# Attention value products: one group per query tile, or one group per branch over up to 512 queries

## The reference, cut to what matters

```python
ss = jnp.einsum('bgrqd,bgqnkd->bgrqnk', qb, k_sel) - slopes[..., None] * d_s
ss = jnp.where(d_s >= 0, ss, NEG)
p_s = jax.nn.softmax(...)
o_s = jnp.einsum('bgrqnk,bgqnkd->bgrqd', p_s, v_sel)
...
return gb[0] * o_c + gb[1] * o_s + gb[2] * o_w
```

## Time and profile before

| | us |
|---|---|
| median of 3 runs (1801.71 to 1802.36) | 1801.89 |
| the profiled execution's own time | 1800.54 |
| its span in the profile | 1798.7 |
| PE busy, share | 1764.1, 98% |
| DVE busy, share | 1222.4, 68% |
| ACT busy, share | 711.9, 40% |
| PE busy in 1290 to 1384 | 83.96 of 94.00 |
| DVE busy there | 79.05 |
| ACT busy there | 74.66 |

### The profile page before, as it was taken

The page is one execution under the profiler, slowest core; times in us unless marked ns, Lnnn a source line. Parts: engine busy times, 40 slices in busy tenths (PEclk is TensorE's granted clock), DMA queues, the critical chain, the costliest instruction groups (busy, mean ns, idle before and its releaser), DMA issues.

```text
span 1798.7 us, 23469 instructions
## 1 busy us (share of the span) xinstructions
PE 1764.1 (98%) x8780; PEld 1426.4 (79%) x8780; DVE 1222.4 (68%) x1784; ACT 711.9 (40%) x964; POOL 164.9 (9%) x40
## 2 busy tenths in 40 slices
PE   7999999999999999999999999999999999999998
PEld 7896888888887988688888888787756878888886
DVE  5367786877877555868886877863787545555556
ACT  5323442332433513353332332646786532222222
POOL 0000000000000000000000000000101344444442
PEclk9999999999999999999999999999999999999999
DMA  6330334333332243123334333253400222222221
GB/s 270 118 114 27 138 110 148 120 117 140 117 121 91 92 131 104 61 105 134 125 122 144 117 117 140 72 173 111 110 13 1 94 71 95 97 101 101 96 94 70
DMA packets 30991, 194.23 MB, mean 108 GB/s; under 512 B 5456, under 2 KB 5840, under 8 KB 8656
## 3 DMA queue, kind: packets, MB, share of 16 engines
q1 hardware_dynamic: 22752, 156.77, 24.9%
q10 hardware_dynamic: 8176, 36.58, 6.1%
HBM read 187.04 MB, written 2.11 MB: 105 GB/s over the span
## 4 chain that ended last, share of the span: by engine, by line
PE 91%; DVE 4%; issue 2%; ACT 2%; DMA 1%; POOL 0%; DVEq 0%; ACTq 0%; SPq 0%; PEldq 0%
PE ps L486 28%; PE ps L488 28%; PE ps L487 28%; PE ps L630 1%; PE ps L644 1%; DMA raw<-in_weights 1%; DVE pb L2218 1%; PE ps L652 0%; PE ps L614 0%; PE ps L899 0%; PE ps L809 0%; DVE wl L1709 0%; DMA x<-in_xin 0%; ACT pt L1480 0%; DVE nt L1677 0%
## 5 line engine op out<-in xcount | busy, mean ns | idle before, releaser
L486 PE MATMUL ps<-xh,wh 128*128 128x512 f32 x1440 | 567.4, 394 | 13.6 <-DVE xl L1662 9.5
L488 PE MATMUL ps<-xh,wl 128*128 128x512 f32 x1440 | 561.4, 390 | 0.0
L487 PE MATMUL ps<-xl,wh 128*128 128x512 f32 x1440 | 561.0, 390 | 0.0
L1057 ACT ACTIVATE wh<-raw 128x2048 fp32r<-128x2048 f32 x143 | 273.6, 1915 | 451.3 <-DMA raw<-in_weights 446.7
L486 PEld LDWEIGHTS ps<-xh,wh 128*128 128x128 f32 x1440 | 270.7, 188 | 73.2 <-issue 14.6
L487 PEld LDWEIGHTS ps<-xl,wh 128*128 128x128 f32 x1440 | 270.9, 188 | 56.8 <-issue 1.7
L488 PEld LDWEIGHTS ps<-xh,wl 128*128 128x128 f32 x1440 | 270.6, 188 | 56.7
L1709 DVE TENSOR_TENSOR wl<-raw,wh 128x2048 fp32r<-128x2048 f32 x109 | 249.0, 2285 | 93.0 <-ACT wh L1057 93.0
L459 POOL TENSOR_TENSOR wl<-raw,wh 128x2048 fp32r<-128x2048 f32 x35 | 161.2, 4608 | 1605.8 <-ACT wh L1057 1507.8
L2307 DVE TENSOR_TENSOR ymix<-ymix,ps 128x512 f32<-128x512 f32 x112 | 74.3, 682 | 149.5 <-PE ps L488 144.8
L486 PE MATMUL ps<-wh,ah 128*128 128x512 f32 x432 | 170.8, 395 | 1.6 <-DVE al L1935 1.2
(11 more groups left out here) (292 smaller groups left out, 2189.4 us busy)
## 6 DMA issues: line engine op xcount, KB each, us to landing
raw<-in_weights SPq DMA_DIRECT2D x144, 1024.0 KB, 4.8
adab<-in_ada ACTq DMA_DIRECT2D x22, 1024.0 KB, 4.8
t<-in_cst ACTq DMA_DIRECT2D x1, 3200.0 KB, 10.3
turned<-q ACTq DMA_DIRECT2D x8, 256.0 KB, 4.0
turned<-k ACTq DMA_DIRECT2D x8, 256.0 KB, 4.1
adab_tail<-in_ada ACTq DMA_DIRECT2D x2, 1024.0 KB, 9.3
out_y<-x SPq DMA_DIRECT2D x8, 256.0 KB, 2.0
raw<-in_weights SPq DMA_DIRECT2D x2, 512.0 KB, 6.6
```

The costliest lines, as they stand in the source:

```text
L486: pe.matmul(out, w_hi, m_hi, start=start, stop=False)
L487: pe.matmul(out, w_hi, m_lo, start=False, stop=False)
L488: return pe.matmul(out, w_lo, m_hi, start=False, stop=stop)
L1057: act.activation(wh[:, s, :], raw[:, s, :], ACT.Copy).then_inc(hi_made, 1)
```

## The change

The transposed weights of one whole branch are kept: `pt` grows from two slots of one unit to one area of four key tiles by 512 queries for each g. It lies over the parts of `xh` and `xl` that hold channels 512 to 1023, whose last readers are the projections ahead of attention. K(U) writes the columns of its query tile. The value products of v = 0 to 3 run as one group behind T of v = 4, those of v = 4 to 7 as one group behind T of v = 8, and the compressed ones, now `compressed_values`, behind T of v = 0 of the next round, where they were. In a group, key tile j takes the queries from j * 128 to 511 in one matmul for each g, so a branch has 8 matmuls (16 records). `pt` may be overwritten only when the group before has read it: K of v = 0 and 4 waits for key tile 0 of that group, K of v = 1 and 5 for all of it (`values_before`).

```diff
+        xh_at = top[0]
         xh = keep("xh", [P, KT, S], F32R)
+        assert top[0] == xh_at + size([P, KT, S])
         xl = keep("xl", [P, KT, S], F32R)
...
-        pt = at("pt", [P, 2, 2, NT, P], F32, big + 28672)
+        pt = at("pt", [P, 2, KT, S], F32, xh_at + size([P, 4, S]))
...
+        def values_before(U):
+
+            r, v = divmod(U, 9)
+            if v == 8:
+                return 5 * r
+            return 5 * r + (0 if v >= 4 else -3) + (1 if v % 4 == 0 else 2)
...
-            def values(U):
-
-                r, v = divmod(U, 9)
-                pe.wait_ge(pt_evac, U + 1)
-                if v == 0 and r >= 2:
+            def values(r, b):
+
+                pe.wait_ge(pt_evac, 9 * r + 4 * b + 4)
+                if b == 0 and r >= 2:
                     pe.wait_ge(att_evac, r - 1)
-                i, b = v % 4, v // 4
-                for j in range(i + 1) if v < 8 else (0,):
+                for j in range(NT):
                     for g, h in enumerate(halves):
-                        if v < 8:
-                            last = pe.matmul(ps[h, 6 + r % 2, i * P:(i + 1) * P], vv[:, j, b * P + HD * g:b * P + HD * g + HD],
-                                             pt[:, U % 2, g, j, :], start=(v == 0), stop=False)
-                        else:
-                            last = pe.matmul(ps[h, 6 + r % 2, :], vcs[0:N_CMP, HD * g:HD * g + HD], ptc[0:N_CMP, g, :],
-                                             start=False, stop=True)
+                        last = pe.matmul(ps[h, 6 + r % 2, j * P:S], vv[:, j, b * P + HD * g:b * P + HD * g + HD], pt[:, g, j, j * P:S],
+                                         start=(b == 0 and j == 0), stop=False)
+                    if j in (0, NT - 1):
+                        last.then_inc(values_used, 1)
+
+            def compressed_values(r):
+
+                pe.wait_ge(pt_evac, 9 * r + 9)
+                for g, h in enumerate(halves):
+                    last = pe.matmul(ps[h, 6 + r % 2, :], vcs[0:N_CMP, HD * g:HD * g + HD], ptc[0:N_CMP, g, :], start=False, stop=True)
                 last.then_inc(values_used, 1)
...
                 turn(U)
-                if U:
-                    values(U - 1)
-            values(UNITS - 1)
+                r, v = divmod(U, 9)
+                if v in (4, 8):
+                    values(r, v // 4 - 1)
+                if U and v == 0:
+                    compressed_values(r - 1)
+            compressed_values(3)
...
                 act.wait_ge(t_done, U + 1)
-                if U >= 2:
-                    act.wait_ge(values_used, U - 1)
+                if v in (0, 1, 4, 5, 8) and values_before(U) > 0:
+                    act.wait_ge(values_used, values_before(U))
                 if v < 8:
-                    w = (v % 4 + 1) * P
-                    act.activation(pt[:, U % 2, :, 0:v % 4 + 1, :], ps[:, 4:6, 0:w].rearrange("p g (j t) -> p g j t", t=P), ACT.Copy)                       .then_inc(pt_evac, 1)
+                    i = v % 4
+                    act.activation(pt[:, :, 0:i + 1, tokens(i)], ps[:, 4:6, 0:(i + 1) * P].rearrange("p g (j t) -> p g j t", t=P), ACT.Copy)\
+                       .then_inc(pt_evac, 1)
...
-                act.wait_ge(values_used, 9 * r + 9)
+                act.wait_ge(values_used, 5 * r + 5)
```

## The result

| us | before | after |
|---|---|---|
| median, 5 runs of each | 1801.89 | 1815.44 |
| lowest to highest | 1801.08 to 1802.57 | 1809.95 to 1815.97 |
| profiled execution's own time | 1800.54 | 1815.97 |

The ratio is 1.0071, with a 95% interval of 1.0059 to 1.0082: **slower by 13.5 us**, where 6.4 were forecast. The sign was right; the forecast size was about half of what was measured, and the median lies outside the stated range of 1803 to 1811. The runs of the changed kernel also scatter: four lie at 1814.6 to 1816.0 with a mean clock of 0.992 or 0.993, one at 1809.95 with 0.996. This clock (the mean of the clock that PE was granted over an execution) is the first thing to read here.

What follows compares the result with a forecast made beforehand. No engine is full: PE, DVE and ACT hand work round a ring, so delays pass on. Four rounds' delays, 1.5 + 1.7 + 1.56 + 1.7 = 6.4 us, on the median 1801.89 gave 1808.3 us, range 1803 to 1811.

Steps and rivals of the forecast that it cites:

- PE's columns stay, a merged group costs 2.30: Value products on PE: 2560 columns a branch before and after; each new group's step 2.30 us, bounds 2.13 and 2.37.
- The first half gains 0.72, the first group gives 0.55 more than that back, T(25) is 0.55 late: Third round: T(22) 0.72 us earlier, then the first merged group makes S(25), and so T(25), 0.55 us later.
- The wait of K(22) for key tile 0 costs nothing: ACT's copy after the first merged group: new wait costed at nothing, up to 0.9 us a round if uncovered.
- the walk: The prediction's start-by-start tracing of one attention round, third round 22.07 us, giving 1.56 us later for that round.
- Taking the value groups out of PE's waiting time ahead of T(25) gives nothing: Third round, M(25) to T(25): PE waits there anyway, so removal saves nothing and the 0.55 us delay goes through.
- The clock rival: Attention's PE waits growing to 1.6 us might lower the clock; unpriced, sharing chance 0.08 with K(22) waiting in earnest.
- The late second group, +1.56 for the round, 6.4 in all: Second merged group between T(26) and S(29): S(29) 1.56 us late in the third round, 6.4 us over four rounds.
- The rival by which PE's saved gaps would show (-4.1): Attention: if DVE and ACT had queued work, 24 saved group gaps would show, -4.1 us, 1797.8; chance 0.08.

Runs made afterwards that it cites:

- late_fill: Changed kernel with each merged value group one score product later, plus useless products ahead of T of v = 7 and in the last round: 1806.60 us.
- fill_v7: Changed kernel plus useless repeats of the next unit's first score product ahead of T of v = 7 (6, last round 7): 1808.17 us.
- less_values: undo_order without the value products of query tiles v = 4, 5 and 6, so one branch's result is incomplete: 1807.02 us, ratio 1.0024.
- spread_both: Against undo_order, both branches use 512-column products, one key tile at a time behind successive units, finished heads copied one unit later: 1806.59 us, ratio 1.0030.
- undo_order: Changed kernel's memory layout with the old order, one value group per query tile: 1801.88 us against 1801.92 before, ratio 1.0001.
- merge_second: Against undo_order, only the second branch of each round merged, one group behind T of v = 8: 1812.36 us, ratio 1.0059.

## Why the prediction was right or wrong, step by step

**PE's columns stay, a merged group costs 2.30.** Right: the step is 2.30 (1355.93 to 1358.23). By the Trainium skill ("TensorE: Matmul & The Clock Gate", Back-to-back issue gap) the merged groups should have become cheaper than the old ones by an estimated 9 us in all. These traces don't agree: no run with the clock held is shorter than before by more than 0.11 us in the stretch.

**The first half gains 0.72, the first group gives 0.55 more than that back, T(25) is 0.55 late.** Right to 0.01 us, in the table above.

**The wait of K(22) for key tile 0 costs nothing.** Right in the changed kernel: its waits list no time of ACT for the merged group, and T(22) to T(25) are as in the walk. late_fill has such waits, 4.2 us in all.

**Taking the value groups out of PE's waiting time ahead of T(25) gives nothing.** This is the step that failed. The prediction costed it at nothing and named the cover, PE waiting there anyway. It was not free: those groups helped to keep the clock up. Without them the clock fell in every round of the profile, T(25), T(26) and the second group ran in part at half pace, and 7.3 us came on top (fill_v7 against the change). less_values shows the same without a merged group. The text on record also names the wrong groups, V(23) and V(24). By its own rows, V(24) stands behind T(25); what stood ahead of T(25) and went is V(22) and V(23).

**The clock rival.** I named the fall of the clock with a chance of less than 0.08, and argued that it holds at 1.00 through waits of 1.4 us and mine grow to 1.6. The longest wait was the wrong number to look at. The profile of before has one wait of 1.41 with the clock up, and less_values one of 1.58; what changed is that the groups between the waits, V(22) and V(23), were gone as well, and a second wait came, 0.51 ahead of T(24). And I gave it no price: three of the four falls of the profile last some 7 us, and PE's matmuls take about twice as long in them.

**The late second group, +1.56 for the round, 6.4 in all.** Right: 23.65 for 23.63 in fill_v7's third round, and 6.25 us in its median. The four rounds of fill_v7's profile are longer than before by 1.6, 1.7, 1.6 and 1.7 us, where the walk had 1.5, 1.7, 1.56 and 1.7 (their sum is 6.46, which the text on record gives as 6.4). The rival by which PE's saved gaps would show (-4.1) had no support in any run.

## What to carry to other kernels

Where engines hand work round a ring, a group's price on PE is what stands behind it in the order: walking one round from start to start gave each start to 0.01 us up to the fall of the clock, and the whole delay to 0.1 us where the clock held. Merging small groups into a block takes them out of waits that they filled for nothing and puts them in front of something that is waited for. And count a removed group that filled a wait as a risk for the clock: look at a whole stretch of PE between two dense ones, not at the longest single wait, and price a fall by the work that follows: in these profiles most falls last about 7 us, several some 3.5, and two, in the last rounds of less_values and spread_both, about 10.

## What the hardware showed that was not expected

Less work can take longer: without 3 of 9 value groups a round the median rose from 1801.7 to 1807.0 us, and with 24 useless records a round the changed kernel fell from 1815.4 to 1808.2. The fall is not a fixed event: undo_order has it ahead of T(34) in its profile and the kernel before has not, with the same wait of 1.41 us; less_values has it in three rounds and merge_second in two of four, with the same waits; and the runs of the changed kernel differ by 6 us among themselves. Most of what was left in the stretch ahead of a fall are transposes and short score products; no run here separates the kind of work from the idle time, so which of the two decides stays open.
